# Starting the mixers on the unscaled stream, and mixing a pair's maps ahead of the next scores

## What is computed

```python
xn = rms_norm(h, norm_mix)              # x * rsqrt(mean(x*x) + eps) * g
pa, pb, pc = split(xn @ w_in)           # q, k, v of three mixers A, B, C
# A: differential attention, 4 heads, two maps each
a = softmax(s[:, 0]) - lam * softmax(s[:, 1]);   o = rms_norm(a @ v, subln_g)
merged = sum(sigmoid(xn @ w_gate[i]) * (y[i] @ w_branch[i]) for i in range(3))
h = h + merged @ w_out
```

## Time and profile before

| what | value |
|---|---|
| median of 3 runs (lowest to highest) | 2229.5 us (2229.28 to 2234.39) |
| the profiled execution | 2229.66 us |
| its span, first to last instruction | 2227.9 us |
| mean granted PE clock | 0.997 |
| PE busy | 2185.4 us, 98% |
| DVE busy | 1221.5 us, 55% |
| ACT busy | 891.9 us, 40% |
| POOL busy | 204.8 us, 9% |

### The profile page before, as it was taken

The page is one execution under the profiler, slowest core; times in us unless marked ns, Lnnn a source line. Parts: engine busy times, 40 slices in busy tenths (PEclk is TensorE's granted clock), DMA queues, the critical chain, the costliest instruction groups (busy, mean ns, idle before and its releaser), DMA issues.

```text
span 2227.9 us, 35632 instructions
## 1 busy us (share of the span) xinstructions
PE 2185.4 (98%) x12372; PEld 1796.9 (81%) x12372; DVE 1221.5 (55%) x2661; ACT 891.9 (40%) x1845; POOL 204.8 (9%) x201
## 2 busy tenths in 40 slices
PE   8999999999999999999999999999999999999998
PEld 6567766778888889999999878887777787888887
DVE  6778786557736755543443455544455665443442
ACT  5566445444424444222232345444344443322332
POOL 0100134310000012000001000010000130000001
PEclk9999999999999999999999999999999999999999
DMA  4111211234533332332333133222243233332332
GB/s 121 39 40 47 60 48 53 81 105 143 153 113 94 102 115 77 93 107 81 91 91 101 58 93 92 67 72 77 67 111 88 82 100 94 94 102 87 94 103 77
DMA packets 375432, 195.66 MB, mean 88 GB/s; under 512 B 42332, under 2 KB 369352, under 8 KB 375324
## 3 DMA queue, kind: packets, MB, share of 16 engines
q1 hardware_dynamic: 374405, 193.84, 30.3%
q10 hardware_dynamic: 919, 0.43, 0.1%
HBM read 191.96 MB, written 11.88 MB: 91 GB/s over the span
## 4 chain that ended last, share of the span: by engine, by line
PE 66%; issue 19%; DVE 3%; ACT 2%; POOL 1%; POOLq 0%; DVEq 0%; ACTq 0%
PE acc L1247 35%; PE acc L1557 17%; PE acc L1297 5%; PE sco L1597 2%; PE acc L1666 1%; PE acc L1662 1%; PE sco L1341 1%; POOL vT L1168 1%; DVE w_lo L2380 1%; PE acc L1388 1%; PE sco L1639 0%; PE sco L1617 0%; PE acc L1639 0%; PE acc L1375 0%; DVE bias L2368 0%
## 5 line engine op out<-in xcount | busy, mean ns | idle before, releaser
L1802 ACT ACTIVATE w_hi<-raw 128x512 fp32r<-128x512 f32 (+4 forms) x656 | 372.2, 615 | 692.3 <-PE acc L1247 658.7
L2380 DVE TENSOR_TENSOR w_lo<-raw,w_hi 128x512 fp32r<-128x512 f32 (+4 forms) x656 | 421.2, 682 | 133.6 <-ACT w_hi L1802 129.0
L1247 PE MATMUL acc<-xn_hi,w_hi 128*128 128x512 f32 (+1 forms) x1408 | 420.0, 339 | 2.1 <-DVE qbuf L2947 2.1
L1247 PE MATMUL acc<-xn_lo,w_hi 128*128 128x512 f32 (+1 forms) x1408 | 421.1, 340 | 0.0
L1247 PE MATMUL acc<-xn_hi,w_lo 128*128 128x512 f32 (+1 forms) x1408 | 420.6, 340 | 0.0
L1247 PEld LDWEIGHTS acc<-xn_hi,w_hi 128*128 128x128 f32 x1408 | 242.2, 188 | 35.7 <-DVE qbuf L2947 3.0
L1247 PEld LDWEIGHTS acc<-xn_hi,w_lo 128*128 128x128 f32 x1408 | 241.8, 188 | 30.0
L1247 PEld LDWEIGHTS acc<-xn_lo,w_hi 128*128 128x128 f32 x1408 | 240.5, 188 | 31.1 <-issue 0.5
L1247 PE MATMUL acc<-hid_lo,w_hi 128*128 128x512 f32 (+1 forms) x832 | 261.5, 349 | 0.0
L1247 PE MATMUL acc<-hid_hi,w_lo 128*128 128x512 f32 (+1 forms) x832 | 260.3, 347 | 0.0
L1247 PE MATMUL acc<-hid_hi,w_hi 128*128 128x512 f32 (+1 forms) x832 | 259.5, 346 | 0.8 <-DVE hid_lo L2889 0.8
(11 more groups left out here) (407 smaller groups left out, 2968.6 us busy)
## 6 DMA issues: line engine op xcount, KB each, us to landing
raw<-in_w_ffn_in SPq DMA_DIRECT2D x176, 256.0 KB, 3.0
raw<-in_w_in SPq DMA_DIRECT2D x118, 256.0 KB, 3.1
raw<-in_w_up SPq DMA_DIRECT2D x88, 256.0 KB, 3.0
raw<-in_w_ffn_out SPq DMA_DIRECT2D x32, 384.0 KB, 3.3
raw<-in_w_gate SPq DMA_DIRECT2D x48, 256.0 KB, 3.1
raw<-in_w_ffn_out SPq DMA_DIRECT2D x32, 320.0 KB, 3.7
raw<-in_w_out SPq DMA_DIRECT2D x32, 256.0 KB, 3.0
lines_dram<-line_dram SPq DMA_DIRECT2D x12, 527.5 KB, 5.4
```

Of the source, the lines that this page charges most:

```text
L1247: mm = pe.matmul(acc[0:m, 2 * slot + b, 0:size], w[slot][:, t, 0:m], x[:, place(t), c:c + size], start=(t == 0 and w is w_hi and x is xh), ...
L1802: act.activation(w_hi[slot][:, a:b, :], raw[slot][:, a:b, :], ACT.Copy).then_inc(S[f"hi_ready{slot}"], parts)
L2380: dve.tensor_tensor(w_lo[slot][:, a:b, :], raw[slot][:, a:b, :], w_hi[slot][:, a:b, :].bitcast(F32), ALU.subtract).then_inc(S[f"split{slot ...
```

## The change

Four things are done.

1. The norm phase is gone, with its 40 bridge matmuls. ("down", 2, 1) now also writes `h * g`, without 1/rms, into `xn_hi` (ACT) and `xn_lo` (DVE) after each of its 8 items, as two other layers of the kernel already do.
2. The mixers begin with three items of 512 columns on that unscaled stream: gate 0, gate 1 and q 0. After gate 0's fifth tile PE sums the squares; ACT's root and DVE's reciprocal follow. Then DVE and ACT make the scaled stream and overwrite `xn_hi` and `xn_lo` tile by tile, each tile as soon as q 0, the last of the three, has used it. k 0 is the first item on the scaled stream. POOL multiplies the three results by 1/rms where they lie, and the two gates get their tanh only then, behind the first "vturn".
3. The order changes up to mixer B: q 1 stands ahead of the first pair, and the gates are shared out as 0 and 1 ahead, 2 and 3 in head 0, one in head 1, one in head 2 and two in head 3 (before: two in each). From mixer B's first k on, the items have the same numbers and order as before.
4. For pairs 3 to 16, DVE runs `mix_maps` of the pair before ahead of `score` of this pair; before, it ran after the value that follows.

Core of the diff:

```diff
-          ("norm", "norm_mix_2", 2), ("mixers",), ("resplit", 2), ("proj_out", 2),
+          ("mixers",), ("resplit", 2), ("proj_out", 2),
-UNSCALED = {("proj_out", 1): GAIN["norm_ffn_g"], ("down", 1, 1): N_VEC, ("proj_out", 2): GAIN["norm_ffn2_2"]}
+UNSCALED = {("proj_out", 1): GAIN["norm_ffn_g"], ("down", 1, 1): N_VEC, ("down", 2, 1): GAIN["norm_mix_2"],
+            ("proj_out", 2): GAIN["norm_ffn2_2"]}
...
+    n = [add(*item) for item in (("gate", "A2", 0), ("gate", "A2", 1), ("q", "A2", 0), ("k", "A2", 0), ("q", "A2", 1),
+                                 ("v", "A2", 0))]
+    dense(n[0], 0, 5)
+    order.append(("root", 0))
+    dense(n[0], 5, KT)
+    order.extend([("scale", k) for k in range(4)])
+    dense(n[1], 0, 5)
+    for t in range(3):
+        dense(n[2], t, t + 1)
+        dense(n[1], 5 + t, 6 + t)
+    order.extend([("scale", 4), ("scale", 5)])
+    dense(n[2], 3, KT)
+    order.extend([("scale", 6), ("scale", 7)])
     dense(n[3], 0, KT)
     dense(n[4], 0, KT // 2)
-    order.append(("vturn", 0))
+    order.append(("pair", 0))
     dense(n[4], KT // 2, KT)
-    order.append(("turn", 0))
+    order.append(("pair", 1))
+    dense(n[5], 0, KT)
...
-        for m in (2 * i, 2 * i + 1):
+        for m in {0: (2, 3), 1: (4,), 2: (5,)}.get(turn, (2 * i, 2 * i + 1)):
...
+                    for j, x in enumerate((gate_of[0], gate_of[1], qbuf[:, 0, META:T])):
+                        pool.wait_ge(S[f"acc_free{j % 2}"], n.at(f"acc_free{j % 2}", k_of_item(j)))
+                        pool.tensor_tensor(x, x, rstd[:, META:T], ALU.mult).then_inc(S["early_scaled"], 1)
...
+                def take_scaled(k):
+
+                    act.wait_ge(S["tmp_ready"], n.at("tmp_ready", k + 1))
+                    if k < KT - 1:
+                        act.wait_ge(S["early_used"], n.at("early_used", k + 1))
+                    else:
+                        act.wait_ge(S["item_done0"], n.at("item_done0", 2))
+                    act.activation(xn_hi[:, k, :], tmp[k % 2], ACT.Copy).then_inc(S["xhi_ready"], 1)
...
                     elif what == "pair":
+                        if 3 <= j <= 16:
+                            mix_maps(j - 1)
                         score(2 * j)
                         score(2 * j + 1)
...
                         take_output(j)
-                        if j + 2 < 16:
-                            mix_maps(j + 2)
-                        elif j == 14:
+                        if j == 14:
```

More of the change, by code:

```diff
@@ L1559, in dense, with sum_squares @@
                                                stop=(t == tiles - 1 and w is w_lo))
+                        if j == EARLY - 1 and t < tiles - 1:
+                            mm.then_inc(S["early_used"], 1)
                     if end == tiles:
                         mm.then_inc(S[f"item_done{slot}"], 1)
+                def sum_squares():
+                    pe.wait_ge(S["sq_added"], n.at("sq_added", 0))
+                    for b, (c, size) in enumerate(segs(2)):
+                        mm = pe.matmul(sco[:, 2 + b, 0:size], ones[:, :], square_sum[:, c:c + size], start=True, stop=True)
+                    mm.then_inc(S["sq_used"], 1)
                 counts = dict(pairs=0, meta=0)
@@ L1695, in mixers @@
                         dense(j, *part)
+                    elif what == "root":
+                        sum_squares()
                     elif what == "pair":
@@ L1705, in mixers @@
                         turn_values(j)
-                    else:
+                    elif what == "oturn":
                         turn_outputs(j)
@@ L1750, in _ @@
                     bridge(14)
[L1751 to L1756, removed]
-                    mm.then_inc(S["sq_used"], 1)
-                    bridge(26)
                 elif kind == "front":
@@ L2076, in take_item @@
                             act.activation(vT[0:64, c], acc[64:P, b, 0:T // 2], ACT.Copy).then_inc(freed, 1)
+                    elif kind == "gate" and j < EARLY:
+                        act.activation(gate_of[at], acc[:, slot, :], ACT.Copy).then_inc(free, 1)
                     elif kind == "gate":
@@ L2156, in mixers @@
                         later = j
+                    elif what == "root":
+                        take_root()
+                    elif what == "scale":
+                        if later is not None:
+                            split_item(later)
+                            later = None
+                        take_scaled(j)
                     elif what == "pair" and j < 2:
@@ L2172, in mixers @@
                         take_values(j)
+                        if j == 0:
+                            early_gates()
                     elif what == "oturn":
@@ L2205, in _ @@
                             x_copied_act, 1)
-                elif kind == "norm":
-                    for ev in ("acc_free0", "acc_free1", "plain_ready"):
-                        act.wait_ge(S[ev], n.at(ev, 0))
-                    norm(ph[1], ph[2])
                 elif kind == "front":
@@ L2816, in mixers @@
                         later = j
+                    elif what == "root":
+                        invert_root()
+                    elif what == "scale":
+                        if later is not None:
+                            split_item(later)
+                            later = None
+                        scale_stream(j)
                     elif what == "pair":
+                        if 3 <= j <= 16:
+                            mix_maps(j - 1)
                         score(2 * j)
```

108 lines of the change are left out of this document (45 added, 63 removed).

## The result

| | before | after |
|---|---|---|
| median of 9 runs | 2230.56 us | 2235.19 us |
| lowest and highest | 2228.44 and 2234.39 us, and one run of 6222.91 | 2233.03 and 2242.03 us |
| profiled execution (span) | 2229.66 us (2227.9) | 2234.5 us (2232.6) |

What follows compares the result with a forecast made beforehand. PE, busy 98% of the span, was taken to bound the kernel. From 2229.66 us, -10.3 + 0.9 - 2.1 + 10.75 + 0.7 + 2.0 = +1.95 gave 2231.6, said as 2231.5, range 2221 to 2238.

Steps and rivals of the forecast that it cites:

- Term 1: Head of the mixers: lost PE time falls from 15.5 to 5.2 us, a gain of 10.3, before POOL's cost of 0.9.
- POOL beside DVE: Head of the mixers: POOL's three multiplications stretch DVE by 1.8 us, half on the path: cost 0.9, between 0 and 4.3.
- Term 2: Head 0: with the mix ahead of the scores, three turns' waits of 0.65 to 0.72 us go, a gain of 2.1.
- Term 3: Ends of the heads: new waits at two turns (2.8 us) and three "oturn" (7.95), a loss of 10.75, bounds 9.0 to 11.5.
- small new waits: Where fewer tiles lie between, PE waits for copied accumulators: 0.7 us, between 0 and 1.5.
- Term 4: Slower clock behind the new waits: 1.1 us behind k 0, about half a fall at another; 2.0 us, 0 to 10.
- The heads' ends do bind: Rival claimed the opposite: DVE reaches the mix early there, only the turns' 2.8 us are lost; 2221.7 us, chance 0.24.
- Clock falls at every wait of 1.3 us: Rival: six falls, behind k 0, two turns and three "oturn", cost 10.2 us in place of 2.0; 2239.8 us, chance 0.14.
- POOL holds DVE: Rival: in the head of the mixers POOL blocks DVE for all of its 4.3 us; 2234.9 us, chance 0.06.
- late mix: Rival: the mix, waiting for exponentials, delays every score and pairs wait, some 0.3 us in 13; 2235.4 us, chance 0.04.

Runs made afterwards that it cites:

- start alone: The changed kernel with maps mixed behind the copied output again, as before the change: 2229.6 us, 1.0003 of the kernel before.
- scaling early: The changed kernel, but DVE scales a head's outputs right behind turns 5, 9 and 13, in its idle time: 2222.83 us, 0.9975 of the kernel before.
- mix alone: The kernel before with only the mixing part, maps mixed ahead of the next scores: 2231.59 us, 1.0015 of the kernel before.
- POOL late: The changed kernel, but POOL waits for the eighth scaled tile before its three multiplications by 1/rms: 2233.07 us, 1.0013 of the kernel before.
- q 0 first: The changed kernel, but q 0 is copied out ahead of the fifth scaled tile, the split between them later: 2229.95 us, 1.0006 of before.

## Why the prediction was near, and where it was off

**Term 1, the head.** Right in its mechanism: no bridge is left, and k 0 waits for `qbuf`'s copy. Against before the lost PE time fell by 15.8 - 8.7 = 7.1 us by the profile (the prediction's working, on the 22.75 us from the last "down" matmul to q 0's start at 1265.57 and the 32.45 to q 1's in the change), where 9.4 was the sum of the term. With the clock held up it would be 9.1, and without POOL's hold on k 0's wait (1.2) the 10.3 of the first estimate. The wait, said to be 3.9 us, was 4.98, and 3.80 with POOL out of the way.

**POOL beside DVE.** Here a step failed, by its reading. I took the earlier trace rows as four scalings stretched by 0.29 us among them, "less than a full block", and so a partial price. The same four by instruction, in the kernel before:

```profile
L2796 DVE TENSOR_SCALAR aux<-aux,stats x4: 275/276/578, 1430.3 to 1431.2; 128x128 f32<-128x128 f32 x4
```

Three took their usual time and one took all of the stretch. The row spoke for standing still, not for sharing. In the change the three splits lose 1.10, 0.67 and 0.68 us, 2.45 of the rival's 4.3; 1.2 of them were on k 0's wait, where I had put 0.9. The Trainium skill's page SBUF — State Buffer, section "SBUF: two separate sides", says that the shared port pair is an exclusive lock and that the other engine fully blocks; the splits of this trace agree (0.694 and then 1.778 us).

**Term 2, the mix.** Right: the three waits of 0.65 to 0.72 are gone.

**Term 3, the heads' ends.** Right in place and size. Turns 9 and 13 wait 1.24 and 1.26 (1.4 said), "oturn" 3.15, 3.16 and 2.04 (3.1, 3.1 and 1.75): new waits of 2.5 + 8.2 = 10.7 us for 10.75. The small new waits came to about 1.1 (the rest of the waits view against the same view of before), for 0.7; the largest of them is 1.03 us at turn 1, which the view puts down to "issue". By the code that turn waits for the scores of the pair ahead of it, and it starts 0.1 us behind the end of DVE's second score:

```profile
1301.42 0.08 DVE L2709 DVE_READ_ACCUMULATOR2_ANT stats<- 128x1 f32 x1
...
1301.61 0.27 PE L1628 MATMUL sco<-const,aux 128*16 128x128 f32 x1 [1.03 <-issue]
```

In the kernel before it starts 0.1 us behind it too (1298.61 and 1298.71, a wait of 0.29), and so do turns 8 and 12 in the change (0.33 and 0.68). The start alone has 1.02 at turn 1, so that wait comes with the start and not with the mix; no run takes it away.

**Term 4, the clock.** This is the term that was mis-sized. I had 2.0 us: 1.1 behind k 0, and half a fall at one of two "oturn". In the profile it is 2.0 behind k 0, by the run with that wait filled, and 1.6 behind "oturn" 1, by the run with those waits filled (193.24 - 191.62): 3.6. Over many runs it is more, since 9 of 15 such waits were followed by a fall, about 1.8 falls in a run or 2 to 3 us, and filling the three waits gave 5 us, give or take 3. The step that failed was "PE is full on both sides, so I don't expect a fall every time": k 0's wait brought one each time. The Trainium skill's page TensorE: Matmul & The Clock Gate, section "What's actually happening", has throttled as the default that activity releases; the trace agrees for k 0, and for "oturn" six waits of 15 went without.

**The sum.** In the profile: -9.1 + 2.0 - 2.1 + 10.7 + 1.6 + 1.1 = +4.2, against 4.5 measured and +1.95 predicted. Of the 2.5 us between, 1.6 are the clock, 0.4 small waits and 0.3 POOL. The median is 4.6 above that of before.

**The rivals.** The heads' ends do bind (scaling early and mix alone). Clock falls at every wait of 1.3 us: not at the turns, always at k 0, often at "oturn"; nearer than the chance of 0.14 said. POOL holds DVE: true as a mechanism, at just over half its price. Its 2234.9 and the late mix's 2235.4 lie nearest to the measured 2235.2, but neither was why. "Late mix" named pairs that wait for scores. No pair does; turns 8 and 12 do, 1.0 us together, where the start alone waits 1.5 for the mix itself.

## What to carry to other kernels

Work that is put ahead in an in-order queue delays all that stands behind it there, not only what one has in mind: ask at each exceptional place (here the end of a head) what else is in the queue, and move the short urgent step into the engine's idle time. Filling a lean stretch with items from later leaves fewer of them to cover the waits there; look at those waits with the filling gone before you book the gain. And price a wait of some microseconds on PE with the slower clock behind it, from more than one execution.

## What I had not expected of the hardware

- After one and the same wait of 3.15 us at "oturn" 0 the granted clock fell in three of four profiles (it did not in the change's own), and it fell behind one of 1.87 us and not behind one of 1.86. The length of the wait alone doesn't decide; one profile shows one draw.
- The lower level behind k 0 lasted 6.8 us in five of six profiles, although PE issued tiles all the time, and 3.4 in POOL late; behind "oturn" always 3.4 us.
- A DVE subtraction of two tiles in SBUF and a POOL multiplication of two tiles stand still for each other: 1.778 us for 0.69 on DVE, 1.794 for 1.285 on POOL, and 3.08 us for a split of 1.29 when two POOL operations came in a row (in q 0 first).
